# A kernel's first stage in another order, with 21 small products of the ones tile in TensorE

## The reference, cut to what matters

```python
mod = silu(cvec) @ ada_w + ada_b                  # 6 blocks of 1024: sh1, sc1, g1, sh2, sc2, g2
h = rmsnorm(x, norm1_w) * (1 + sc1) + sh1
proj = h @ w_in                                   # q, ff, fb, iv, g, hy
...
h = sin(fr1 * (feats @ w1 + b1)); h = sin(fr2 * (h @ w2 + b2)); h = h @ w3
h = h * exp(-t * deltas)                          # the filter's taps, forward and backward
kern = kern / (sum(abs(kern), axis=0) + EPS)
z = irfft(rfft(u) * rfft(kern)) + hy_d * u
...
x = x + g1 * (merged @ w_out)
x = x + g2 * convffn(rmsnorm(x, norm2_w) * (1 + sc2) + sh2)
```

## Time and profile before

| what | value |
|---|---|
| median of 3 runs | 972.93 us (971.53 to 974.05) |
| the profiled execution | 974.58 us |
| its span | 972.8 us, 13784 instructions |
| PE busy | 927.6 us (95% of the span) |
| DVE busy | 623.8 us (64%) |
| ACT busy | 340.3 us (35%) |
| POOL busy | 17.2 us (2%) |
| chain that ended last | PE 75%, DVE 15%, ACT 3%, DMA 3% |
| moved by DMA | 99.36 MB, mean 102 GB/s |

### The profile page before, as it was taken

One profiled execution on the slowest core, in us unless ns is written; L12 is line 12 of the kernel. 1 busy time (PEld: TensorE's weight loads), 2 busy tenths in 40 slices (PEclk: granted clock), 3 DMA queues, 4 the chain that ended last, 5 costly groups with the idle time before them and its releaser, 6 DMA issues.

```text
span 972.8 us, 13784 instructions
## 1 busy us (share of the span) xinstructions
PE 927.6 (95%) x5594; PEld 820.1 (84%) x5594; DVE 623.8 (64%) x818; ACT 340.3 (35%) x599; POOL 17.2 (2%) x26
## 2 busy tenths in 40 slices
PE   4897999999999999999999999999999999999996
PEld 1256989898898898688789899888999988999985
DVE  4553565785875985699586766544666644566665
ACT  2624343343425333323373333311333321233332
POOL 0000000100000001002000000000000000000000
PEclk9999999999999999999899999999999999999999
DMA  7456341342244254317221222222122222122102
GB/s 271 169 181 202 114 131 65 130 137 93 87 152 136 58 180 140 87 51 160 100 82 45 91 68 85 87 81 71 65 82 71 66 96 78 65 67 86 44 1 108
DMA packets 34503, 99.36 MB, mean 102 GB/s; under 512 B 3768, under 2 KB 12088, under 8 KB 33673
## 3 DMA queue, kind: packets, MB, share of 16 engines
q1 hardware_dynamic: 31672, 89.15, 27.6%
q0 software_dynamic: 2768, 9.33, 3.9%
HBM read 95.31 MB, written 3.16 MB: 101 GB/s over the span
## 4 chain that ended last, share of the span: by engine, by line
PE 75%; DVE 15%; ACT 3%; DMA 3%; issue 2%; SPq 1%; ACTq 0%; DVEq 0%
PE ps L1473 21%; PE ps L1475 21%; PE ps L1474 21%; DMA raw<-in_slots 3%; PE ps L1686 3%; PE ps L1491 2%; DVE w_lo L984 2%; PE ps L1552 1%; SPq L550 1%; DVE o_hg L1215 1%; PE ps L1698 1%; PE ps L1827 1%; DVE KK L1175 1%; ACT w_hi L661 1%; PE ps L1706 1%
## 5 line engine op out<-in xcount | busy, mean ns | idle before, releaser
L1473 PE MATMUL ps<-h_hi,w_hi 128*128 128x320 f32 x1152 | 360.7, 313 | 7.0 <-ACT padf L666 2.9
L1475 PE MATMUL ps<-h_hi,w_lo 128*128 128x320 f32 x1152 | 355.9, 309 | 0.0
L1474 PE MATMUL ps<-h_lo,w_hi 128*128 128x320 f32 x1152 | 355.9, 309 | 0.0
L1473 PEld LDWEIGHTS ps<-h_hi,w_hi 128*128 128x128 f32 x1152 | 216.5, 188 | 8.4 <-issue 3.4
L1474 PEld LDWEIGHTS ps<-h_lo,w_hi 128*128 128x128 f32 x1152 | 216.5, 188 | 0.1
L1475 PEld LDWEIGHTS ps<-h_hi,w_lo 128*128 128x128 f32 x1152 | 216.3, 188 | 0.0
L984 DVE TENSOR_TENSOR w_lo<-raw,w_hi 128x1024 fp32r<-128x1024 f32 x106 | 129.5, 1225 | 117.2 <-ACT w_hi L661 113.8
L661 ACT ACTIVATE w_hi<-raw 128x1024 fp32r<-128x1024 f32 x106 | 110.9, 1053 | 102.1 <-PE ps L1475 91.6
L1474 PE MATMUL ps<-w_lo,a_hi 128*128 128x512 f32 x220 | 85.6, 389 | 0.0
L1473 PE MATMUL ps<-w_hi,a_hi 128*128 128x512 f32 x220 | 85.6, 389 | 0.0
L1475 PE MATMUL ps<-w_hi,a_lo 128*128 128x512 f32 x220 | 85.6, 389 | 0.0
(11 more groups left out here) (260 smaller groups left out, 1030.0 us busy)
## 6 DMA issues: line engine op xcount, KB each, us to landing
raw<-in_slots SPq DMA_DIRECT2D x138, 512.0 KB, 3.7
raw<-in_slots SPq DMA_DIRECT2D x32, 256.0 KB, 6.6
xin<-in_x_sample SPq DMA_DIRECT2D x4, 512.0 KB, 10.5
grow<-gates POOLq DMA_DIRECT2D x2, 1024.0 KB, 12.8
x<-in_x_sample POOLq DMA_DIRECT2D x2, 1024.0 KB, 13.7
out_y_sample<-x SPq DMA_DIRECT2D x4, 512.0 KB, 3.1
decay<-in_decay SPq DMA_DIRECT2D x1, 1280.0 KB, 8.1
ktab<-in_ktab SPq DMA_DIRECT2D x1, 1024.0 KB, 8.8
```

The source lines that it names most:

```text
L1473: mm(out, lhs[0], rhs[0], start=first, stop=False)
L1474: mm(out, lhs[0], rhs[1], start=False, stop=False)
L1475: return mm(out, lhs[1], rhs[0], start=False, stop=last)
```

## The change

The first stage runs in another order. The loads of hcol and w2 go to ScalarE's queue, those of w3, decay, ktab and ptab_k to GpSimd's; the pieces of ada 1 no longer go through the ring but into buffers that lie on those of the splits of units 2 and 3 (`apart`), which wait for their use. The range reduction of the sine has three instructions in place of seven, with the frequencies scaled beforehand and the factor 2 pi in ScalarE's sine. A first small Sin loads its table ahead. The sum of the taps' sizes is taken later: three of its five tiles are added by GpSimd, and TensorE sums twice (`tap_sums`) in place of five times. The absolute values, `make_knorm`, and the splits of units 1 to 3 stand at other places. Between the value steps the transposes and the modulation parts 2 and 3 are distributed anew. And `keep_busy` multiplies the ones tile with itself (128x128) into a bank that is free then: 5 times before the first hidden layer's product, 8 times behind it, 8 times behind the second's.

```diff
+RINGED = (0, 2, 3)
 def stream():
-    for e in range(ADA_EARLY):
-        out += [("ada", e, q) for q in range(PIECES)]
-        if e < 2:
-            out.append(("weight", e))
-    out += [("weight", n) for n in range(2, IV + HEAD_TILES + LEAD)]
+    for e in RINGED:
+        out += [("ada", e, q) for q in range(PIECES)] + [("weight", len(out) // 5)]
+    out += [("weight", n) for n in range(len(RINGED), IV + HEAD_TILES + LEAD)]
...
+        lead_hi = sb(lead, "lead_hi", [2, UNIT])
+        lead_lo = sb(lead, "lead_lo", [2, UNIT])
-        ADA_BANK = (2, 3, 7, 7) + (3,) * (len(ADA_ORDER) - ADA_EARLY)
-        V_BANKS = (0, 2, 1, 3, 4)
+        ADA_BANK = (2, 3, 5, 7) + (3,) * (len(ADA_ORDER) - ADA_EARLY)
+        V_BANKS = (0, 2, 3, 4, 1)
+        def size_free(n):
+            return (sem("size_added"), n - 2) if n > 2 else (sem("size_max"), 1)
 # SyncE
-            (hcol, w2, w3, decay)
             fetch(0, 4)
-            (ktab, ptab_k)
             for i in range(NT):
                 load(xin[:, i, :], x_rows(i), f"ld_x{i}")
-            fetch(4, len(STREAM))
+            fetch(4, 5)
+            for q in range(PIECES):
+                load_pair(apart(q), APART, q, f"ld_apart{q}")
+            fetch(5, len(STREAM))
 # GpSimd
             load(vec[:, :], io["vec"], "ld_vec")
+            (w3 in two loads, decay)
             load(ident[:, :], io["ident"], "ld_ident")
+            (ktab, ptab_k)
+            total = feats[:, 0:HW]
+            for n in range(1, NT - 1):
+                eng.wait_ge(sem("size_max"), n + 1)
+                if n > 1:
+                    eng.wait_ge(sem("size_added"), n - 1)
+                nc.gpsimd.tensor_tensor(total, total, sizes(n)[:, 0, :], ALU.add).then_inc(sem("size_added"), 1)
 # ScalarE
+            (hcol and w2, two loads of each)
             A(silu_c ...)
+            A(stat[:, 2, 0, 0:1], eps[:, :], ACT.Sin)
+            for i in range(2):
+                eng.wait_ge(sem("arg_ready"), i + 1)
+                A(hid[:, i, :], arg[:, 1, :], ACT.Sin, scale=-TURN).then_inc(sem("hid_ready"), 1)
             A(bound[:, 1, :], bound[:, 0, :], ACT.Exp).then_inc(sem("bound_exp"), 1)
-            tap_abs(0) ada_row(0) tap_abs(1) norm1(0) tap_abs(2) take_odd(0) tap_abs(3) norm1(1) tap_abs(4)
-            norm1(2) norm1(3) take_odd(1) sums_row norm1(4) split_hi(0) take_odd(2) modulate(0) modulate(1)
-            take_odd(3) ada_row(1) split_hi(1) modulate(2) modulate(3) ada_row(2) split_hi(2)
-            modulate(4) modulate(5) ada_row(3) modulate(6) modulate(7) split_hi(3)
+            ada_row(0) norm1(0) norm1(1) norm1(2) take_odd(0) norm1(3) norm1(4) take_odd(1) split_hi(0)
+            modulate(0) modulate(1) take_odd(2) tap_abs(0) tap_abs(1) ada_row(1) tap_abs(2) tap_abs(3)
+            take_odd(3) tap_abs(4) split_hi(1) ada_row(2) sums_row modulate(2) to modulate(5)
+            ada_row(3) modulate(6) modulate(7) split_hi(2) split_hi(3)
 # VectorE
-                link(V.tensor_scalar(q, a, 1.0 / two_pi, 12582912.0, ALU.mult, ALU.add))
-                link(V.tensor_scalar(q, q, 12582912.0, None, ALU.subtract))
-                for cc in (c1, c2, c3):
-                    link(V.scalar_tensor_tensor(out=a, in0=q, scalar=-cc, in1=a, op0=ALU.mult, op1=ALU.add))
-                link(V.tensor_scalar(a, a, -3.1415925, 3.1415925, ALU.max, ALU.min), "arg_ready")
+                link(V.tensor_scalar(q, a, 12582912.0, None, ALU.add))
+                link(V.scalar_tensor_tensor(out=q, in0=q, scalar=12582912.0, in1=a, op0=ALU.subtract, op1=ALU.subtract), "arg_ready")
-            damp(0) to damp(3) tap_size(0) tap_size(1) damp(4) tap_size(2) to (4) sum_groups(0) gain_pair(0)
-            scale_x(0) scale_x(1) join(0) scale_x(2) scale_x(3) join(1) make_knorm() scale_x(4) split_lo(0)
-            join(2) split_h(0) split_h(1) join(3) kspec_p sum_groups(1) gain_pair(1) split_lo(1) split_h(2)
-            split_h(3) sum_groups(2) gain_pair(2) split_lo(2) split_h(4) split_h(5) sum_groups(3)
-            gain_pair(3) split_h(6) split_h(7) split_lo(3)
+            damp(0) to damp(4) sum_groups(0) gain_pair(0) bound scale_x(0) scale_x(1) scale_x(2) join(0)
+            scale_x(3) scale_x(4) join(1) split_lo(0) split_h(0) split_h(1) join(2) tap_size(0) tap_size(1)
+            sum_groups(1) gain_pair(1) tap_size(2) tap_size(3) join(3) kspec_p tap_size(4) split_lo(1)
+            sum_groups(2) gain_pair(2) split_h(2) split_h(3) make_knorm() split_h(4) split_h(5)
+            sum_groups(3) gain_pair(3) split_h(6) split_h(7) split_lo(2) split_lo(3)
 # TensorE
+            def keep_busy(n):
+                for _ in range(n):
+                    mm(ps[:, 7, 0:P], ones[:, :], ones[:, :], start=True, stop=True)
+            def tap_sums():
+                eng.wait_ge(sem("size_max"), NT)
+                eng.wait_ge(sem("size_added"), NT - 2)
+                mm(ps[0:GROUP, 1, :], ones[:, 0:GROUP], feats[:, 0:HW], start=True, stop=True)
+                mm(ps[GROUP:2 * GROUP, 1, :], ones[:, 0:GROUP], sizes(NT - 1)[:, 0, :], start=True, stop=True).then_inc(sem("tap_summed"), 1)
+            keep_busy(5)
             (the first hidden layer)
+            keep_busy(8)
             (the second hidden layer)
-            ada_quad(0, 0)
+            keep_busy(8)
             tap_pair(0)
             first_tap(1, 0, (slice(0, NHID),) * 2)
-            ada_quad(0, 1) tap_pair(2) ada_turn(0) tap_prompt() tap_sum(0) tap_sum(1) filter_dft(0) tap_sum(2)
-            tap_sum(3) filter_dft(1) tap_sum(4) filter_dft(2) (turn of the sums) (x: k = 0, 1) filter_dft(3)
-            ada_quad(1, 0) ada_quad(1, 1) (prompt's transform) ada_turn(1)
+            ada_quad(0, 0) tap_pair(2) ada_quad(0, 1) tap_prompt() ada_turn(0) filter_dft(0) filter_dft(1)
+            (x: k = 0, 1) filter_dft(2) ada_quad(1, 0) ada_quad(1, 1) filter_dft(3) ada_turn(1)
+            (prompt's transform)
 # TensorE, x_between: behind value step at = 5 * p + i
-            1: x 2, 3    3: ada_quad(2)    5: ada_turn(2)    6: x 4, 5    7: sample 6, ada_quad(3), sample 7
-            8: ada_turn(3)    9: prompt 6, 7
+            0: ada_quad(2)    1: ada_turn(2), tap_sums    2: prompt 2 to 5, sample 2, 3, turn of the sums
+            5: sample 4, 5    6: ada_quad(3)    7: sample 6, ada_turn(3)    8: sample 7, prompt 6, 7
```

More of the change, by code:

```diff
@@ L550, in load, with load_pair @@
                 eng.dma_start(dst, src).then_inc(sem(name), 16)
+            def load_pair(dst, e, q, name):
+                for what in range(2):
+                    s, at = ada_pair(e, what, q)
+                    src = io["slots"][s, :, at - at % UNIT:at - at % UNIT + UNIT].rearrange("p (k c) -> p k c", k=2)
+                    load(dst.rearrange("p (k w c) -> p k w c", k=2, w=2)[:, :, what, :],
+                         src[:, :, at % UNIT:at % UNIT + PAIR], name)
             def fetch(r0, r1):
@@ L563, in fetch @@
                     if kind == "ada" and which[0] < ADA_EARLY:
[L564 to L568 removed]
+                        load_pair(raw[:, r % RING, :], *which, f"raw_in{r % RING}")
                         continue
@@ L613, in _ @@
             load(vec[:, :], io["vec"], "ld_vec")
+            for rows in (slice(0, NHID), slice(NHID, P)):
+                load(w3[rows, :], io["hy_w3"][0], "ld_w3")
+            load(decay[:, :, :], io["decay"], "ld_decay")
             load(ident[:, :], io["ident"], "ld_ident")
+            load(ktab[:, :, :, :, :], io["ktab"], "ld_ktab")
+            load(ptab_k[:, :, :], io["ptab"][:, 0], "ld_ktab")
+            total = feats[:, 0:HW]
[4 more added lines that the diff above has]
+                nc.gpsimd.tensor_tensor(total, total, sizes(n)[:, 0, :], ALU.add).then_inc(sem("size_added"), 1)
             eng.wait_ge(sem("h_split"), KD)
@@ L762, in _ @@
             modulate(7)
+            split_hi(2)
             split_hi(3)
@@ L1107, in join @@
                 link(V.tensor_tensor(kspec[:, m, 1, cs, :], first, second, ALU.subtract), "kspec_ready")
-            for n in range(4):
+            for n in range(NT):
                 damp(n)
+            sum_groups(0)
+            gain_pair(0)
+            eng.wait_ge(sem("bound_exp"), 1)
+            link(V.reciprocal(bound[:, 2, :], bound[:, 1, :]))
+            link(V.tensor_tensor(bound[:, 2, :], bound[:, 1, :], bound[:, 2, :], ALU.mult))
+            link(V.tensor_tensor(bound[:, 3, :], bound[:, 2, :], bound[:, 2, :], ALU.subtract))
+            link(V.tensor_scalar(bound[:, 4, :], bound[:, 3, :], -1.0, 1.0, ALU.mult, ALU.add))
+            scale_x(0)
+            scale_x(1)
+            scale_x(2)
+            join(0)
+            scale_x(3)
+            scale_x(4)
+            join(1)
+            split_lo(0)
+            split_h(0)
+            split_h(1)
+            join(2)
             tap_size(0)
             tap_size(1)
-            damp(4)
-            for n in range(2, NT):
-                tap_size(n)
-            sum_groups(0)
-            gain_pair(0)
-            scale_x(0)
```

(16 more changed lines are left out.)

201 lines of the change are left out of this document (94 added, 107 removed).

## The result

The changed kernel takes 968.83 us as the median of 11 runs (966.41 to 970.94), beside 972.93 (971.53 to 976.03) for the kernel before: a ratio of 0.995, with a 95% interval of 0.9937 to 0.9963. It is faster, by 3.6 to 6.1 us. Forecast were 962 and at most 968, so the sign was right and the size was not: the time lies 0.8 us outside the range, and less than half of the forecast gain came. The profiled execution took 968.83, with a span of 967.0 against 972.8 of the one before: 5.8 us. That is more than the 4.1 us between the medians, since the profiled execution of the kernel before lies 1.65 us above its median and that of the changed kernel lies at its own.

The account below looks back on a forecast made before the run. TensorE, busy 95% of the span, bounds it; only its idle or removable work can go. First half product 12.7 us earlier, less 1.6 of clock, is 11.1 off 974.58: 963.5, or 962 as median; range 958 to 968.

Parts of the forecast that it names:

- the landmark: Start of the first half product on TensorE, forecast to move from 88.32 to 75.6 us, all behind it moving along.
- A: Stage start up to the first tap product: 18.76 us becomes 11.5.
- The rise of the clock "at 5.6": TensorE, working nearly without a break from 1.1 us, was taken to reach its full rate at 5.6 us.
- B: The taps, from first tap product to first filter transform: 13.1 us becomes 11.8.
- bound (1): decay's landing: at 11.8 us it gives 0.7 us more gain, at 17 it gives 2.3 less.
- R2: Rival: GpSimd's queue partly late, decay at about 18 to 25 us, gain 1 to 8, time 965 to 972; 15%.
- C: From first filter transform to first value product: 27.2 us becomes 21.2, including 1.5 of wait for the scaled tokens.
- bound (3): GpSimd's three additions, estimated at twice VectorE's 0.69 us; at four times, 0.3 us lost at most.
- D: From first value product to first half product: 29.2 us becomes 31.1, with 23.1 of work plus waits, 4.1 at the end.
- I take the same loss there: Clock fall behind the longer idle before the first half product, taken to lose 1.6 us as in the old kernel.
- R3: Rival: the ones products do nothing for the clock and stand in the way, time 965; 10%.

Follow-up runs that it names:

- the kernel with the ring held: Changed kernel, but SyncE waits for hcol and w2 before issuing the first ring piece: 966.12 us, ratio 0.994 to the kernel before.
- the kernel with the early split: Changed kernel with split_hi(2) ahead of modulate(6) and split_lo(2) ahead of split_h(6): 960.37 us, ratio 0.9887 to the kernel before.
- The kernel with both moves: Changed kernel with make_knorm ahead of split_h(2), and unit 2's split ahead of modulate(6) and split_h(6): 957.4 us, ratio 0.9841 to the kernel before.

## Why the prediction was wrong, step by step

- **The reading that the stage is what changes, and the landmark as its measure: right.** The rest of the program stayed within 2 us in every kernel. What I left out is that its clock falls differ from run to run, by 1.7 us and more, and that the runs of one kernel spread by up to 7 us.
- **A, the step that failed first.** "The 4 loads that ScalarE issues (0.6 each, as on SyncE) end near 3.2, before vec arrives at 3.88, and cost nothing." The issues do end at 3.2, but I priced the issue and not the landing. In the kernel before, w3, decay and the ring stood behind hcol and w2; moving w3 and decay to GpSimd and starting the ring at 1.6 put two large streams beside them. hcol at 7.85 instead of 4.8 lets the first sine begin at 9.75 and end at 10.28, where the prediction had the first hidden layer at 7.6. w2 was there at 9.8, and so by its landing would have held the second hidden layer (10.42) nearly as long even with an early hcol; the prediction has no wait for it. The gap moves the second sine from a forecast end of 11.4 to 14.28; the slower second hidden layer (1.54 us instead of 0.74) is a part of that, and the last eight products, at the lower rate at first, hold the tap to 14.79. With both loads sooner, in the kernel with the ring held, the first tap comes at 12.24, which is 2.55 of the 3.3 us. Of these 3.3, 1.05 is the clock's and not the loads': with the same loads and the same idle the kernel with the early split has its first tap at 13.74.
- **The rise of the clock "at 5.6": wrong, near 14.** The last eight products took 2.97 us, between 3.78 and the 2.05 of later kernels. TensorE was not nearly without a break; the break of 1.67 us was the consequence of the late loads. But without any break, in the kernel with the ring held, the full rate came only near 9 too. Yet the first tap pair ran at full rate, 1.99 us, as I had said, and not at 2.8.
- **B, 11.8: right**, 11.1. decay, there at 13.4, never became the limit; bound (1) and R2 had no case. (The prediction's 14.7 for it is a slip: 1.8 MB from 4 us on, at half of 0.37 MB/us, is 13.7.)
- **C, 21.2: right**, 20.6, with a wait of 1.79 for the scaled tokens (1.5 forecast).
- **GpSimd's additions, bound (3): right.** They took 1.27, 1.80 and 1.29 us (the estimate was twice 0.69):

```profile
43.16 1.27 POOL L645 TENSOR_TENSOR feats<-feats,decay 128x512 f32<-128x512 f32 x1 [38.00 <-DVE decay L1110]
46.89 1.80 POOL L645 TENSOR_TENSOR feats<-feats,size 128x512 f32<-128x512 f32 x1 [2.46 <-DVE size L1110]
48.84 1.29 POOL L645 TENSOR_TENSOR feats<-feats,decay 128x512 f32<-128x512 f32 x1
```

  ScalarE waited 1.02 and 2.73 us for them, TensorE not at all. The Trainium skill (GPSIMD Engine Reference, Elementwise — side-by-side cycle accounting) has 1.96 times VectorE's time; the trace has 1.84 with VectorE idle beside it, 1.87 with VectorE copying for most of it, and 2.6 while VectorE adds tiles itself (46.85 to 49.0).
- **D, the waits right, the sum 2.5 too small.** The kernel with both moves has D without falls of the clock: 46.46 to 72.10 is 25.6, less waits of 0.55 and 0.47 it is 24.6 of work where I summed 23.1 (its terms give 23.2): 1.5 mis-sized in the steps and turns. A value step takes 1.46 to 1.5 us where it stands behind a turn (50.90 to 52.39 in the changed kernel), and 1.4 was taken for all ten. The changed kernel's D has 7.2 of waits (8.0 forecast), so 26.4 is left, 1.8 more than 24.6: the fall behind the 2.14 us. The prediction put "2.6 before the last value tile" into its sum as a wait alone and priced the clock once for the whole stage. That is the second failed step.
- **The clock, "I take the same loss there", 1.6: mis-sized**, 2.65. An idle of 4.03 to 4.05 us stands before the half products in seven of the profiled executions, and the loss behind it is 1.7 to 2.9 us; what sets its length no run shows.
- **R3, the products do nothing: wrong.** They are worth 1.2 to 2.0 us at the landmark, in three pairs of profiled executions, and 1.6 to 2.4 in the medians.
- **Together:** 3.3 (A) and 2.5 (D), less 0.7 (B) and 0.6 (C), are the 4.5 us by which 80.16 misses 75.6; with 1.05 more of clock behind it that is 5.6 of the 11.1, and leaves 5.5. The span's gain was 5.8. The medians have 4.1: the 1.65 us by which the profiled execution of the kernel before lies above its median were taken off the forecast as if they were in both kernels, and the changed kernel's profiled execution lies at its median. Where the 1.65 us come from is open.

In the profiled executions the change gains mostly by its order: the landmark moves by 8.2 us, of which the products are 1.45. In the times this is not shown, since the kernel without the products is level with the kernel before within its interval. Which of the other parts (the shorter range reduction, the ring freed from ada 1, the later sums) brings how much was read from the landmarks and not tried one by one.

## What to carry to other kernels

Price a moved load by its landing beside what will now be in flight, not by its issue or by its size: 1 KB was there at 4.8 us with no large stream ahead of it or beside it, at 5.9 to 6.5 beside one large stream and at 7.5 to 8.6 beside two, and letting a large stream wait for it cost nothing, where that stream had slack. In this kernel an idle of TensorE of 2.14 us cost itself and, in seven executions of eight, 1.7 us behind it, and one of 4.05 cost 1.7 to 2.9 behind it; so count each such wait with its fall of the clock, put the last split of a weight ahead of work that nobody waits for yet, and where a wait can't go, small products in it keep the rate. Before comparing two profiled executions, take out the stretches of lower clock that lie where both kernels are the same, and look at how far each lies from the median of its kernel.

## What the runs showed that was not expected

- The clock column does not show the lower rate at the start of the program. With the ring held, it reads 1.00 from 0 us on, while eight products of the ones tile take 3.78 us and the same eight take 2.05 later; here the rate is read from the durations. The window:

```profile
6.00:8.00 2.00, 2.00 (x11) 2.00 (x11) 1.83 (x5) 0.07 (x1) 0.00 (x0) 1.00 0.92 359
```

- The start of the same program does not run the same way twice. Eight products of the ones tile behind the second hidden layer took 2.05, 2.97, 3.15 or 3.68 us in kernels that are alike up to there, as the clock had risen, had not, or had fallen again.
- hcol at 11.09 from the head of SyncE's own queue, against 7.85 from ScalarE's: a place ahead of the ring's pieces was the worse one.
- Falls of the clock followed idles shorter than I thought could matter: 2.14 us in the stage, and in the middle of the program 1.32 us, just behind ten products with one column each. In the changed kernel, TensorE in order of time:

```profile
458.51 1.17 PE L1895 MATMUL ps<-ones,sq 128*128 128x1 f32 x10
461.01 0.79 PE L1504 MATMUL ps<-w_hi,h_hi 128*128 128x512 f32 x1 [1.32 <-DVE h_lo L1370]
461.60 0.63 PE L1505 MATMUL ps<-w_lo,h_hi 128*128 128x512 f32 x1
```

  Behind the last idle a product takes 0.63 us instead of 0.39 for 3.4 us. No kernel here tried to fill that place.
